# Routing from centred rows, and outputs between the chunks: three edits to a two-layer trunk

## The reference

```python
h = layer_norm(ALPHA * h + mix, ln_g[layer, 0], ln_b[layer, 0])
ffn = grouped_moe(h, router_w, router_bias, ...)     # scores = softmax(h @ router_w)
h = layer_norm(ALPHA * h + ffn, ln_g[layer, 1], ln_b[layer, 1])

def layer_norm(x, g, b):
    return (x - mu) * rsqrt(var + LN_EPS) * g + b
```

## Time and profile before

| what | value |
|---|---|
| median of 3 runs | 1307.79 us (1307.54 to 1307.90) |
| the profiled execution, its span | 1310.27 us, 1308.5 us |
| PE / DVE / ACT / POOL busy | 91% / 71% / 53% / 15% |
| chain of waits by engine | PE 80%, DVE 9%, DMA 5%, issue 2%, ACT 2%, POOL 2% |
| mean granted PE clock | 0.949 |
| last V unit to first gate unit (four attention heads) | 112.48 to 172.04 us |
| last projection unit to first gathered rows, layer 0 | 268.4 to 304.48 us |
| the same in layer 1 | 934.4 to 972.29 us |

### The profile page before, as it was taken

One profiled execution on the slowest core, in us unless ns is written; L12 is line 12 of the kernel. 1 busy time (PEld: TensorE's weight loads), 2 busy tenths in 40 slices (PEclk: granted clock), 3 DMA queues, 4 the chain that ended last, 5 costly groups with the idle time before them and its releaser, 6 DMA issues.

```text
span 1308.5 us, 14917 instructions
## 1 busy us (share of the span) xinstructions
PE 1190.7 (91%) x5712; PEld 950.3 (73%) x5713; DVE 922.6 (71%) x1327; ACT 691.4 (53%) x846; POOL 191.0 (15%) x145
## 2 busy tenths in 40 slices
PE   7998899957999999996899999999849999999991
PEld 5785478855888888875787766778737888888870
DVE  5243645656999999987624545674777999999885
ACT  4322324225777777773224544563237777777751
POOL 1000010110222212213001000000211122222103
PEclk9999899967999999999799999999859999999996
DMA  7131013066999999997013420321448999999951
GB/s 269 65 129 65 1 36 126 33 256 218 342 366 371 380 366 369 372 341 268 2 65 114 144 82 17 108 87 65 187 192 315 363 364 377 374 376 365 369 205 64
DMA packets 64876, 281.46 MB, mean 215 GB/s; under 512 B 11510, under 2 KB 11766, under 8 KB 40226
## 3 DMA queue, kind: packets, MB, share of 16 engines
q1 hardware_dynamic: 48672, 247.48, 50.0%
q0 software_dynamic: 12288, 28.42, 7.5%
q10 hardware_dynamic: 3842, 4.57, 1.0%
HBM read 270.91 MB, written 25.20 MB: 226 GB/s over the span
## 4 chain that ended last, share of the span: by engine, by line
PE 80%; DVE 9%; DMA 5%; issue 2%; ACT 2%; POOL 2%; POOLq 0%; DVEq 0%; SPq 0%
PE ps L685 22%; PE ps L687 21%; PE ps L686 21%; DMA ring<-in_moe_w_up_dram 2%; DVE ring_r L1469 2%; PE ps L798 2%; PE ps L734 2%; PE ps L1056 2%; PE ps L1066 2%; PE ps L679 1%; PE ps L1079 1%; PE ps L807 1%; DMA ring<-in_kv_w_dram 1%; DVE arena L1890 1%; DMA arena<-h_rows,tokv 1%
## 5 line engine op out<-in xcount | busy, mean ns | idle before, releaser
L1469 DVE TENSOR_TENSOR ring_r<-ring,ring_r 128x2048 fp32r<-128x2048 f32 x128 | 291.8, 2286 | 6.8 <-ACT ring_r L1221 6.5
L1221 ACT CAST ring_r<-ring 128x2048 fp32r<-128x2048 f32 x128 | 241.4, 1928 | 9.8 <-DMA ring<-in_moe_w_gate_dram 9.2
L686 PE MATMUL ps<-ring_r,xgT_r 128*128 128x512 f32 x528 | 207.5, 393 | 0.0
L1221 ACT CAST high_r<-ring 128x2048 fp32r<-128x2048 f32 x64 | 121.8, 1914 | 94.1 <-DMA ring<-in_moe_w_up_dram 94.1
L1469 DVE TENSOR_TENSOR ring_r<-ring,high_r 128x2048 fp32r<-128x2048 f32 x64 | 146.1, 2294 | 26.4 <-ACT high_r L1221 25.9
L571 POOL DMA_INDIRECT sum_rows<-arena,tokv x28 | 58.4, 2086 | 392.5 <-ACT arena L1271 392.5
L686 PEld LDWEIGHTS ps<-ring_r,xgT_r 128*128 128x128 f32 x528 | 100.4, 190 | 19.1
L685 PE MATMUL ps<-ring_r,xgT_r 128*128 128x512 f32 x272 | 109.0, 401 | 0.0
L685 PE MATMUL ps<-high_r,xgT_r 128*128 128x512 f32 x256 | 104.4, 408 | 2.8 <-DVE xgT_r L1673 2.8
L687 PE MATMUL ps<-ring_r,xgT_r 128*128 128x512 f32 x272 | 106.0, 390 | 0.0
L685 PE MATMUL ps<-featT,ring_r 128*128 128x512 f32 x256 | 103.9, 406 | 0.0
(11 more groups left out here) (262 smaller groups left out, 2220.5 us busy)
## 6 DMA issues: line engine op xcount, KB each, us to landing
ring<-in_moe_w_gate_dram SPq DMA_DIRECT2D x64, 1024.0 KB, 10.9
ring<-in_moe_w_up_dram SPq DMA_DIRECT2D x64, 1024.0 KB, 12.7
ring<-in_moe_w_down_dram SPq DMA_DIRECT2D x64, 1024.0 KB, 11.9
ring<-in_gla_w_in_dram SPq DMA_DIRECT2D x6, 2048.0 KB, 8.0
ring<-in_kv_w_dram SPq DMA_DIRECT2D x4, 2048.0 KB, 13.7
ring<-in_fox_w_qg_dram SPq DMA_DIRECT2D x4, 2048.0 KB, 7.9
ring<-in_gla_w_out_dram SPq DMA_DIRECT2D x2, 2048.0 KB, 7.9
h_rows<-arena POOLq DMA_DIRECT2D x8, 512.0 KB, 6.4
```

Of the source, the lines that this page charges most:

```text
L686: pe.matmul(o, left[0], right[1], start=False, stop=False)
L1221: act.copy(high, w).then_inc(half_high, 1)
L1469: dve.tensor_tensor(low, w, high.bitcast(F32), ALU.subtract).then_inc(half_low, 1)
```

## The change

1. *Order of the attention.* The first `decay_sums`, exponentials and products are moved ahead of the last two V units. `decay_sums(h + 1)` moves behind head h's products. Chunk sums and outputs of a head alternate. The output copies go from DVE to ACT. The split of the weight quarter stands behind the squares on ACT, and stays at its place on DVE. The exponentials' table is loaded earlier. PE's wait for the last copies moves into `tail`.
2. *Router logits.* PE turns the rows of H that are centred and multiplied by g, not yet scaled by the deviation and not shifted. The logits are multiplied by the deviation in `router`, and a shift `ln_b @ router_w` per layer is added; it is made once, from three small loads, two DVE products and eight matmuls ahead of the last two V units. The router's weights are loaded with rows in natural order, in pieces of 64 bytes.
3. *Last tile.* DVE scales the first three tiles as before. The last tile is multiplied by the deviation on ACT and shifted on GpSimd, which clears the pads before that. ACT's multiplication of the last tile by ALPHA moves into `router`. Additions and statistics are taken per half (`rows_normed`).

```diff
+                    if n == 3:
+                        sp.dma_start(shift_w, router_w.rearrange("(q k) n -> q k n", q=P)).then_inc(shift_loaded, 16)
+                        for L in range(DEPTH):
+                            sp.dma_start(shift_col[:, L, :], ln_b[L, 0:1, :].rearrange("a (q k) -> q (a k)", q=P)
+                                         ).then_inc(shift_loaded, 16)
...
+            def clear_pads(L):
+                pool.wait_ge(h_stored, 64 * L + 48)
+                pool.wait_ge(h_scaled, T * L + 2)
+                for n in range(2):
+                    pool.memset(xg[:, n, :], 0.0).then_inc(pads_clear, 1)
...
+                    if s == T:
+                        clear_pads(N // 2)
+                        pool.wait_ge(row_scaled, N // 2 + 1)
+                        rows = blocks(Hp[:, T - 1, :], K)
+                        pool.tensor_tensor(rows, rows, dealt(ln_p[:, 1, :], K), ALU.add).then_inc(ln_ready, 1)
...
+                    if s == T - 1:
+                        pe.wait_ge(o_ev, 4 * H_A)
...
-                for s in range(T + 2):
-                    if s < T:
-                        pe.wait_ge(tp_dve, 2 * (4 * TP_MIX[L] + s + 1))
-                        unit(u0 + 8 + 2 * s)
-                        unit(u0 + 9 + 2 * s, frees=2 if s == T - 1 else 0)
-                    logits(L, s)
-
-            def logits(L, s):
-
-                if s >= 2:
-                    pe.wait_ge(tp_dve, 2 * (4 * TP_RT[L] + s - 1))
-                    mm = narrow(s - 2, rw)
-                    if s == T + 1:
-                        mm.then_inc(rt_logits, 1)
-                if 1 <= s <= T:
-                    pe.wait_ge(ln_ready, 2 * L * T + s)
-                    transpose_tile(TP_RT[L], s - 1, Hp)
+                for t in range(T):
+                    pe.wait_ge(tp_dve, 2 * (4 * TP_MIX[L] + t + 1))
+                    unit(u0 + 8 + 2 * t)
+                    if t >= 1:
+                        turn_centred(L, t - 1)
+                    unit(u0 + 9 + 2 * t, frees=2 if t == T - 1 else 0)
+                    if t >= 1:
+                        logits(L, t - 1)
+                turn_centred(L, T - 1)
+                logits(L, T - 1)
+
+            def turn_centred(L, t):
+                pe.wait_ge(rows_centred, T * L + t + 1)
+                transpose_tile(TP_RT[L], t, H)
+
+            def logits(L, t):
+                pe.wait_ge(tp_dve, 2 * (4 * TP_RT[L] + t + 1))
+                mm = narrow(t, rw)
+                if t == T - 1:
+                    mm.then_inc(rt_logits, 1)
 
...
+            def chunk_states(h, t):
+                if t == 0:
+                    if h == 0:
+                        pe.wait_ge(*taken(U_GLA_TAIL - 2))
+                        pe.wait_ge(*taken(U_GLA_TAIL - 1))
+                    else:
+                        pe.wait_ge(st_done, 7 * h - 1)
+                    pe.wait_ge(kt_ev, h + 1)
+                elif t == 1:
+                    pe.wait_ge(att_ev, h + 1)
+                else:
+                    pe.wait_ge(st_done, 7 * h + 2 * t - 2)
+                for c in range(CPT if t < T - 1 else 1):
+
+                    mm = pe.matmul(ps[:, KV_BANKS[t % 2] + c, 0:DV],
+                                   k_tok[c * CH:(c + 1) * CH, t, :],
+                                   mix[c * CH:(c + 1) * CH, t, h * DV:(h + 1) * DV], start=True, stop=True)
+                mm.then_inc(kv_done, 1)
...
+                if u == U_GLA_TAIL - 2:
+                    pe.wait_ge(shift_in, 2)
+                    pe.wait_ge(z_min, T)
+                    pe.wait_ge(z_abs, T)
+                    for k in range(K):
+                        mm = pe.matmul(ps[:, 6, 0:DEPTH * E], one[:, :].to_broadcast([P, P]),
+                                       shift_prod[:, k, :, :].rearrange("p a e -> p (a e)"),
+                                       start=k == 0, stop=k == K - 1)
+                    mm.then_inc(shift_done, 1)
+                    decay_sums(0)
+                unit(u, frees=1 if u % T == T - 1 else 0)
...
+                if h + 1 < H_A:
+                    decay_sums(h + 1)
+                chunk_states(h, 0)
+                for t in range(1, T):
+                    chunk_states(h, t)
+                    head_output(h, t - 1)
+                head_output(h, T - 1)
...
+            for m in range(8):
+                unit(U_OUT + m, frees=2 if m == 7 else 0)
+                if m in (3, 4, 6):
+                    turn_centred(1, (3, 4, 6).index(m))
+                if m in (5, 6, 7):
+                    logits(1, m - 5)
+            turn_centred(1, T - 1)
+            logits(1, T - 1)
...
-            act.dma_start(raw[1], router_w.rearrange("(q k) n -> q k n", q=P)).then_inc(par_loaded, 16)
+            act.dma_start(raw[1], router_w.rearrange("(k p) n -> p k n", p=P)).then_inc(par_loaded, 16)
...
-                    act.mul(dealt(H[:, t, :], K), blocks(Hp[:, t, :], K), ALPHA).then_inc(h_scaled, 1)
+                    if t < T - 1:
+                        scale_residual(L, t)
+                act.wait_ge(ln_rstd, 2 * L * T + T)
+                act.mul(blocks(Hp[:, T - 1, :], K), dealt(H[:, T - 1, :], K), ln_r[:, T - 1, 1:2]
+                        ).then_inc(row_scaled, 1)
+
+            def scale_residual(L, t):
+                act.wait_ge(ln_ready, 2 * L * T + t + 1)
+                act.mul(dealt(H[:, t, :], K), blocks(Hp[:, t, :], K), ALPHA).then_inc(h_scaled, 1)
...
+                scale_residual(L, T - 1)
...
+            take(U_GLA_TAIL - 3)
             exps(0)
+            take(U_GLA_TAIL - 1)
+            own.settle(act)
             for h in range(H_A):
                 if h + 1 < H_A:
                     exps(h + 1)
-                split(gla0 + 5, range(h, h + 1))
                 for t in range(T):
+                    act.wait_ge(o_done, 4 * h + t + 1)
+                    act.copy(mix[:, t, h * DV:(h + 1) * DV], ps[:, 6 + t % 2, 0:DV]).then_inc(o_ev, 1)
                     act.wait_ge(o_ev, 4 * h + t + 1)
                     if 4 * h + t:
                         act.wait_ge(sq_done, 4 * h + t)
                     act.activation(squares, mix[:, t, h * DV:(h + 1) * DV], ACT.Square,
                                    accum_out=ssq[:, t * H_A + h:t * H_A + h + 1]).then_inc(sq_done, 1)
+                split(gla0 + 5, range(h, h + 1))
...
+            def rows_normed(L, order):
+
+                N = 2 * L
+                done = []
+                for u, p, t in order:
+                    dve.wait_ge(proj_done, u + 1)
+                    hp = H[:, t, p * BANK:(p + 1) * BANK]
+                    dve.scalar_tensor_tensor(out=hp, in0=hp, scalar=ALPHA, in1=ps[:, bank_of(u), :],
+                                             op0=ALU.mult, op1=ALU.add).then_inc(ev_dve, 1)
+                    dve.wait_ge(*taken(u))
+                    own.mark(dve.bn_stats(ln_bn[:, t, p, :], hp))
+                    if done:
+                        s = done.pop(0)
+                        take_tile(TP_RT[L], s)
+                        if s < 2:
+                            low_half(L, s)
+                    if p == 1:
+                        own.settle(dve)
+                        spread(t)
+                        dve.wait_ge(lnp_loaded, 32 * (N + 1))
+                        dve.scalar_tensor_tensor(out=H[:, t, :], in0=H[:, t, :], scalar=ln_mv[:, t, 0:1],
+                                                 in1=ln_p[:, 0, :], op0=ALU.subtract, op1=ALU.mult
+                                                 ).then_inc(rows_centred, 1)
+                        if t < T - 1:
+                            dve.wait_ge(rows_centred, T * L + t + 1)
+                            scale(N, t)
+                        done.append(t)
+                take_tile(TP_RT[L], T - 1)
...
-                do(dve.tensor_copy(logits, halves[:, :, 1, :]))
-                do(dve.tensor_tensor(logits, halves[:, :, 0, :], logits, ALU.add))
+                do(dve.tensor_reduce(logits, halves.rearrange("p t a e -> p t e a"), AX.X, ALU.add))
+                dve.wait_ge(ln_rstd, 2 * L * T + T)
+                do(dve.tensor_tensor(logits, logits, over_e(ln_r[:, :, 1]), ALU.mult))
+                do(dve.tensor_tensor(logits, logits, each_t(shift_logits[:, L, :], E), ALU.add))
...
+            dve.wait_ge(shift_loaded, 16 * (DEPTH + 1))
+            for L in range(DEPTH):
+                dve.tensor_tensor(shift_prod[:, :, L, :], shift_w,
+                                  shift_col[:, L, :].unsqueeze(2).to_broadcast([P, K, E]), ALU.mult
+                                  ).then_inc(shift_in, 1)
+            take(U_GLA_TAIL - 4)
+            dve.wait_ge(shift_done, 1)
+            dve.tensor_copy(shift_logits[:, :, :], ps[:, 6, 0:DEPTH * E].rearrange("p (a e) -> p a e", a=DEPTH)
+                            ).then_inc(shift_ready, 1)
...
-                for t in range(T):
-                    dve.wait_ge(o_done, 4 * h + t + 1)
```

(1 more changed line is left out.)

118 lines of the change are left out of this document (35 added, 83 removed).

## The result

The changed kernel takes **1297.67 us** (median of 4 executions, 1297.51 to 1298.76), the kernel before 1307.85 beside it: a ratio of 0.9923, 95% interval 0.9906 to 0.994. It is faster, by 10.2 us. I had predicted 1283.4 and a range of 1276 to 1295, so the direction is right and the gain is less than half of the 24.4. Its profiled execution took 1297.71 us, with a span of 1296.0 (before: 1308.5) and a mean granted clock of 0.952.

What follows compares the result with a forecast made beforehand. TensorE held four fifths of the chain of waits, so gains lay where it leaves the dense matmuls: 11 + 6.0 + 7.4 = 24.4 us off the profiled 1310.27 gave 1285.9, less 2.5 for the median 1283.4; range 1276 to 1295.

Steps and rivals of the forecast that it cites:

- A, the attention: First GLA attention: reordered heads and output copies on ACT bring the first gate unit earlier, gain 11 us, bounds 6 and 13.
- B: Layer 0, end of output projection to the first expert's turned rows: 30.1 us against 36.1, gain 6.0 us.
- C: Layer 1, end of output projection to the first expert's turned rows: 30.5 us against 37.9, gain 7.4 us.
- E': End of the last output projection unit in the changed kernel, forecast 2.6 us later than before.
- Logits at E' + 8.4: Router: last tile's logits ready 8.4 us after the projection's end, bounds 7.4 to 9.8, with a clock fall inside the last group.
- 13.6 to the gather: Router: from logits to first gather 13.6 us, against 13.4 before, for one more small DVE operation.
- the store's leg: Last tile's store through GpSimd, the other path to the gather: lands at E' + 20.5 to 22.3, a tie, nothing added.
- The gather's 5.5: First gather of token rows: 5.5 us against 4.76 before, overlapping more of ACT's four row stores.
- both cost nothing: Early loads: the shift's three small loads and the router weights' 64-byte pieces were claimed to delay nothing, cost zero.
- the clock still falls: Rival, attention: PE's clock falls twice as before, attention gain only 6 us, time 1288; chance 0.15.
- the heads came closer: Rival, attention, denied this: ACT-to-DVE weight chunk handing takes longer, gain 6.3 us at best, time 1291; chance 0.07.
- the slower case: Rival, attention: PE's clock stays at 1.2 GHz through all four heads, 24 us lost there, time 1318; chance 0.04.

## Why the prediction was wrong, and where it was right

**A, the attention (11): right**, at 11.2. The start of the transposes, the links that set the period and the clock's return are as told. That it came out so near is in part luck: the four heads took 0.9 us more than summed (44.7 for 43.8), and the 1.0 set aside for the clock wasn't needed in this profile, while it falls in the fourth head in five of nine profiles of this code. The terms of the period, added again, give 11.1 and not 11.2. And the size of it holds only against the profiled execution of before, which contained 4.7 us of falls. Against the same code without one (145.5 us from the first marker to the gate's, 138.7 in the changed kernel) A is 6.8.

**The step from the profiled execution to the median: wrong by 2.4.** I took the 24.4 us off 1310.27 and then another 2.5, the distance of that execution from its median, as if the changed kernel's profile had to lie as far above its own median. It lies on it (1297.71 and 1297.67). Part of that distance was probably the falls, whose going A had already counted; no run splits it.

**B (6.0) came to 0.4, and C (7.4) with the loop ahead of it to 0.2.** This is where the gain went, 12.8 us of it, by terms of the sum, layer 0 and layer 1:

- *Logits at E' + 8.4*: 9.4 and 10.1, so 1.0 and 1.7 too little. I had the fall inside the last group; it came ahead of it, within my bounds (7.4 to 9.8) once, outside once. Filled, it was 8.6.
- *13.6 to the gather*: 16.5 and 15.8, so 2.9 and 2.2. This is the step that failed. "One more small DVE operation" was counted, and what GpSimd's new addition does to VectorE was not; I had looked at that addition only as part of the store's leg. The page "SBUF — State Buffer" of the Trainium skill (section "Who interferes with whom") says just this: an operation of VectorE with two operands in SBUF and one of GpSimd that reads SBUF exclude each other, an operation of GpSimd that only writes lets it pass, one of VectorE with a single operand outside the two-port modes passes, and one in those modes excludes GpSimd's. The traces agree (2.84 for 0.22 us under the addition; 0.17 under the memset; 0.22 for a reduction under the addition; 2.50 for 1.66 and 0.88 for 0.17 for operations with a scalar under the memset), though none shows in which mode an operation ran. The page would have changed the sum, and I did not weigh it.
- *The gather's 5.5*: 7.1 and 6.8, so 1.6 and 1.2. I named the stores of the sums and gave them 0.7; seven transfers fell together, which the move of the norm's loads behind the last store brought about. I had costed that move at nothing.
- *The loop between*: from layer 0's turned rows to layer 1's E', 634.9 us against 632.9 by the forecast (934.34 - 304.48 of the earlier trace rows, and the 3.0 of the new order). Later profiles of the same code had 632.6 to 635.3. That is 2.1 here, and its cause stays open.

These make 5.5 and 7.2. With the 2.4 above, less 0.2 from A and 0.7 gained behind layer 1's rows, they are 14.2 of the 14.3 us between forecast and median.

**The start ("both cost nothing"): wrong**, though it cost the first profile only 0.1 us: 1.6 to 3.6 in the eight others. I had asked only whom the 64-byte pieces delay as data, and not what issuing them does to the engine that issues them, nor what PE's longer wait does to its clock.

**The store's leg: right.** The gather was released by the copy of the tables (VectorE's L1746), as the forecast said. The addition was done at E' + 17.2 (17), the store issued at E' + 17.5 (17.5) and landed at E' + 20.9 (20.5 to 22.3). That this is 5 us before the gather, and no tie, comes from the other leg, which stood at E' + 25.9 in place of 22.0. The addition took 2.84 us with its step of 32 bytes, 2.34 without. The page "GPSIMD Engine Reference" of the Trainium skill (section "Performance pitfalls for Q7 kernels") puts such a step at half as much again. The measurement decides: a fifth to a quarter (2.84 and 2.90 to 2.34), for an addition of which one of the two operands has the step. The forecast's estimate by the page was also added wrongly: 1.2 us later in each layer would pass the logits' leg by up to 1.5 each, so up to 3 us, and not 2.

Of the rivals, "the clock still falls" holds in more than half of the profiles of this code, at 1.3 to 4.5 us and not twice; the heads came closer as promised; the slower case had no sign.

## What to carry to other kernels

When a step moves to GpSimd, look up what VectorE runs at that moment. In these traces an operation with two operands waited for the end of GpSimd's addition, and one with a scalar for the end of a memset; on a serial path of 0.2 us steps that is a loss of all that was left of it. When a path gets shorter, list the transfers whose issue did not move with it: they now fall into the transfer that ends the path. And before a gain is taken off the median, see whether the profiled execution holds a disturbance that the gain already counts.

## What I had not expected of the hardware

A load in 1024 pieces of 64 bytes holds the issuing engine for 2.9 to 3.3 us, or makes the next two issues on its list take 1.15 to 2.11 us each in place of 0.5; the same bytes in 512-byte pieces took 0.50. A gather of 512 KB went from 4.8 to 7.1 us behind 3.5 MB of other transfers issued within 8.6 us; 2.5 MB did not slow it, and neither did the 3.5 MB with four of the transfers begun 4.5 us earlier. PE's clock fell after a single wait of 2.4 us in 5 of 9 executions of the same instructions, and with the wait filled or cut to 0.8 in none of 6; at the start it fell in 10 of 12 after a wait of 2.4 to 3.2 us and in none of 6 after 1.65 to 1.81.
